# A hybrid encoder layer on one core: x parked in eight pieces, row factors broadcast from a column over the identity

## The reference

```python
h = rmsnorm(x, g_mix_pre)
q_a, k_a, v_a, q_r, k_r, v_r, g_r, gate_a, gate_r = split_in(h @ w_in)
o_a = sink_attention(...)          # 8 heads of 64, window of 2 chunks, sinks
o_r = head_group_norm(retention(...)) * silu(g_r)     # 4 heads, keys 128, values 256
merged = sigmoid(gate_a) * (o_a @ w_branch_attn) + sigmoid(gate_r) * (o_r @ w_branch_ret)
x = x + rmsnorm(merged @ w_out, g_mix_post)
h = rmsnorm(x, g_ffn_pre)
f = (silu(h @ w_ffn_gate) * (h @ w_ffn_up)) @ w_ffn_down      # hidden 2816
x = x + rmsnorm(f, g_ffn_post)
x = x + (p @ w_ple_proj) * sigmoid(x @ w_ple_gate)
```

## Time and profile before

| | |
|---|---|
| median of three runs | 1070.39 us (1069.06 to 1074.13) |
| the profiled execution | 1072.61 us, of it in the span 1070.8 us |
| busy: TensorE, VectorE, ScalarE, GpSimd | 1031.8, 509.0, 333.2, 127.6 us |
| mean granted clock of TensorE | 0.982 |
| chain that ended last, shares | PE 85%, DVE 6%, issue 3%, DMA 3%, ACT 1%, POOL 1% |
| DMA | 88.63 MB, mean 83 GB/s |

### The profile page before, as it was taken

One profiled execution on the slowest core, in us unless ns is written; L12 is line 12 of the kernel. 1 busy time (PEld: TensorE's weight loads), 2 busy tenths in 40 slices (PEclk: granted clock), 3 DMA queues, 4 the chain that ended last, 5 costly groups with the idle time before them and its releaser, 6 DMA issues.

```text
span 1070.8 us, 19780 instructions
## 1 busy us (share of the span) xinstructions
PE 1031.8 (96%) x7428; PEld 996.9 (93%) x7428; DVE 509.0 (48%) x869; ACT 333.2 (31%) x490; POOL 127.6 (12%) x148
## 2 busy tenths in 40 slices
PE   7999999999999999989969999999999999999797
PEld 6899899898999999989958999999999999999697
DVE  5544676666566433243276443332233444323842
ACT  5224434334334322123333222221123222222232
POOL 0221212122100000100222111100011111011000
PEclk9999999999999999989989999999999999999799
DMA  6732212212221323523221223222332222223132
GB/s 170 229 91 77 67 46 69 61 52 59 69 65 59 90 71 90 151 72 98 78 59 40 79 82 94 74 67 81 93 99 78 78 80 84 69 81 98 40 101 66
DMA packets 163817, 88.63 MB, mean 83 GB/s; under 512 B 14224, under 2 KB 162096, under 8 KB 163648
## 3 DMA queue, kind: packets, MB, share of 16 engines
q1 hardware_dynamic: 160256, 79.19, 25.7%
q0 software_dynamic: 1632, 7.23, 2.0%
q10 hardware_dynamic: 1888, 1.64, 0.5%
HBM read 82.08 MB, written 6.03 MB: 82 GB/s over the span
## 4 chain that ended last, share of the span: by engine, by line
PE 85%; DVE 6%; issue 3%; DMA 3%; ACT 1%; POOL 1%; DVEq 0%; SPq 0%; ACTq 0%; POOLq 0%
PE acc L467 77%; DMA raw<-in_w_in 2%; PE small L618 2%; PE small L633 1%; DMA raw<-in_w_branch_ret 1%; DVE wide L1412 1%; DVE wlo L1101 1%; PE small L661 1%; PE small L665 1%; DVE yl L1428 1%; PE small L663 1%; ACT whi L790 1%; PE small L570 0%; ACT prob L850 0%; PE small L673 0%
## 5 line engine op out<-in xcount | busy, mean ns | idle before, releaser
L1101 DVE TENSOR_TENSOR wlo<-raw,whi 128x1024 fp32r<-128x1024 f32 (+3 forms) x156 | 180.5, 1157 | 337.7 <-ACT whi L790 337.4
L790 ACT ACTIVATE whi<-raw 128x1024 fp32r<-128x1024 f32 (+3 forms) x156 | 153.1, 982 | 436.2 <-PE acc L467 418.9
L467 PE MATMUL acc<-yh,whi 128*128 128x288 f32 x960 | 209.0, 299 | 18.0 <-DVE yl L1428 10.5
L467 PE MATMUL acc<-yh,wlo 128*128 128x288 f32 x960 | 207.9, 298 | 0.0
L467 PE MATMUL acc<-yl,whi 128*128 128x288 f32 x832 | 179.2, 297 | 0.0
L467 PEld LDWEIGHTS acc<-yh,whi 128*128 128x128 f32 x960 | 155.6, 191 | 21.5 <-DVE yl L1428 12.2
L467 PE MATMUL acc<-xh,whi 128*128 128x288 f32 x736 | 163.9, 304 | 3.0 <-DVE wlo L1101 2.9
L467 PE MATMUL acc<-xl,whi 128*128 128x288 f32 x736 | 158.0, 296 | 0.0
L467 PE MATMUL acc<-xh,wlo 128*128 128x288 f32 x736 | 157.5, 295 | 0.0
L467 PEld LDWEIGHTS acc<-yh,wlo 128*128 128x128 f32 x960 | 155.5, 191 | 0.0
L467 PEld LDWEIGHTS acc<-yl,whi 128*128 128x128 f32 x832 | 135.5, 191 | 0.0
(11 more groups left out here) (218 smaller groups left out, 1115.2 us busy)
## 6 DMA issues: line engine op xcount, KB each, us to landing
raw<-in_w_in SPq DMA_DIRECT2D x92, 256.0 KB, 3.1
raw<-in_w_ffn_gate SPq DMA_DIRECT2D x44, 256.0 KB, 3.1
raw<-in_w_ffn_up SPq DMA_DIRECT2D x44, 256.0 KB, 3.2
raw<-in_w_ffn_down SPq DMA_DIRECT2D x48, 192.0 KB, 2.4
raw<-in_w_branch_ret SPq DMA_DIRECT2D x16, 256.0 KB, 2.8
raw<-in_w_out SPq DMA_DIRECT2D x16, 256.0 KB, 2.8
raw<-in_w_ple_gate SPq DMA_DIRECT2D x16, 256.0 KB, 3.0
x_scratch<-x_t POOLq DMA_DIRECT2D x1, 2304.0 KB, 15.5
```

What stands on the lines that cost most here:

```text
L467: ins = nc.tensor.matmul(acc[:, a, hf, 0:HALF], w[:, s, at:at + P], x(k)[:, hf * HALF:(hf + 1) * HALF], start=first and n == 0 and m == 0, ...
L790: nc.scalar.activation(whi[:, s, 0:n], raw[:, s, 0:n], ACT.Copy).then_inc(hi_ready, 1)
L1101: nc.vector.tensor_tensor(wlo[:, s, 0:n], raw[:, s, 0:n], whi[:, s, 0:n].bitcast(F32), ALU.subtract).then_inc(lo_ready, 1)
```

## The change

Two things change. The first is how x is parked: eight transfers, one for each tile, instead of one, issued later in GpSimd's list, and the reload of tile k waits for k units of the second merge stage instead of none. With it, the loads of p and of the caches go ahead of `power(0)`, behind a wait for x's last quarter. The second is the row factor: TensorE uses a column of `rstd`, read 128 times with a step of zero, as the stationary operand and the identity as the moving one. The product has the same values, since its k-th partition holds `rstd[k]` in every column.

```diff
             def row_factor(n):
 
+                pe.wait_ge(rstd_ready, n + 1)
                 for r in range(RT):
                     size = P if r < RT - 1 else DEC
-                    pe.wait_ge(diag_ready, RT * n + r + 1)
-                    ins = nc.tensor.matmul(small[:, r * P:r * P + size], ones[0:size, :],
-                                           diag[0:size, P * r:P * r + size], start=True, stop=True)
-                    ins.then_inc(bcast_done, 1)
+                    ins = nc.tensor.matmul(small[:, r * P:r * P + size], rstd[0:size, r:r + 1].to_broadcast([size, P]),
+                                           ident[0:size, 0:size], start=True, stop=True)
+                ins.then_inc(bcast_done, 1)
...
-                act.wait_ge(bcast_done, RT * (n + 1))
+                act.wait_ge(bcast_done, n + 1)
...
                 if t == 0:
-                    act.wait_ge(x_saved, 16)
+                    act.wait_ge(x_saved, 16 * KD)
...
-                dve.wait_ge(rstd_ready, n + 1)
-                for r in range(RT):
-                    size = P if r < RT - 1 else DEC
-                    nc.vector.tensor_scalar(diag[0:size, P * r:P * r + size], ident[0:size, 0:size],
-                                            rstd[0:size, r:r + 1], None, ALU.mult).then_inc(diag_ready, 1)
...
-            power(0)
+            pool.wait_ge(x_in[QUARTERS - 1], 32)
             pool.dma_start(p_row[:, 0:RT - 1, :], p_p[0, 0].rearrange("(r p) n -> p r n", p=P)).then_inc(p_in, 16)
             pool.dma_start(p_row[0:DEC, RT - 1, :], p_s[0, 0]).then_inc(p_in, 16)
             pool.dma_start(ck_row[:, :], cache_k[0, 0].rearrange("n h d -> n (h d)")).then_inc(cache_in, 16)
             pool.dma_start(cva[:, :], cache_v[0, 0].rearrange("n h d -> n (h d)")).then_inc(cache_in, 16)
+            power(0)
...
-            pool.wait_ge(xt_copied, KD)
-            pool.dma_start(scratch, x_t[:, :, :].rearrange("p k n -> p (k n)")).then_inc(x_saved, 16)
+
+            def save_x(k):
+
+                if k == 0:
+                    pool.wait_ge(xt_copied, KD)
+                pool.dma_start(scratch[:, k * ROWS:(k + 1) * ROWS], x_t[:, k, :]).then_inc(x_saved, 16)
+
...
                     head_job(t, h, slot)
+                    if isinstance(h, int):
+                        save_x(t + 2)
                     pieces(2 * t + 1, r, rslot)
...
             pool.wait_ge(tables_in, 32)
+            save_x(0)
+            save_x(1)
             head(0, None, 0, None)
...
-            pool.wait_ge(unit_done, U_MRG2)
-            pool.wait_ge(x_saved, 16)
+            pool.wait_ge(x_saved, 16 * KD)
             for k in range(KD):
+                pool.wait_ge(unit_done, U_MRG2 + k)
                 pool.dma_start(res[:, k, :], scratch[:, k * ROWS:(k + 1) * ROWS]).then_inc(x_back, 16)
```

More of the change, by code:

```diff
@@ L293, in encoder_layer @@
         assert e_at + slab + ROWS * 4 <= split_at
-        diag = tb
         acc = ctx.enter_context(nc.psum_tensor("acc", [P, 2, 2, 512], F32))
@@ L318, in encoder_layer @@
         x_saved, x_back = sem("x_saved"), sem("x_back")
-        squares_ready, var_ready, rstd_ready, diag_ready = (
-            sem("squares_ready"), sem("var_ready"), sem("rstd_ready"), sem("diag_ready"))
+        squares_ready, var_ready, rstd_ready = sem("squares_ready"), sem("var_ready"), sem("rstd_ready")
         bcast_done, rb_ready, sums_done = sem("bcast_done"), sem("rb_ready"), sem("sums_done")
@@ L1160, in _ @@
                 if k == 1:
-                    dve.wait_ge(bcast_done, RT)
+                    dve.wait_ge(bcast_done, 1)
                 nc.vector.tensor_copy((ta, tb)[k][:, :], small[:, 1024 * (k % 2):1024 * (k % 2) + ROWS]).then_inc(xt_copied, 1)
```

## The result

The changed kernel takes 1062.28 us in the median of 4 runs (1061.99 to 1062.63), the kernel before 1070.52 in the 4 runs beside them (1069.06 to 1074.13). The ratio is 0.9925, 95% interval 0.9911 to 0.994: 8.2 us less. The two profiled executions took 1072.61 and 1061.99; the trace accounts for the 10.8 us between their spans, which is more than the medians differ by.

A forecast was written before the change was run, and what follows sets the result against it. TensorE, busy 1031.8 of 1070.8 us, bounds the kernel; only its pauses and low clock can pay. Parking 2.8, reload 5.9 and row factors 1.1 sum to 9.8 us off the 1070.39 median: 1060.6, eight-in-ten range 1057.0 to 1066.0.

The forecast's parts named there:

- Reload: Late place, w_branch_ret load at 445.7 us: staged reloads save 3.5 us pause plus 2.4 low clock, 5.9 us.
- The price of 0.9 us per piece: Second merge: each of eight reload pieces delayed the late weight load by 0.9 us, also used for head 0.
- Row factors: Four row factors: dropping 20 VectorE multiplications and their hand-over saves 0.45, 0.4, 0 and 0.3, sum 1.1 us.
- The weight load with a step of zero: Row factors: cost taken as 0; the rival that zero-step loads are slow, up to 4.5 us, 1065.1, chance 0.05.
- Parking: Early place, w_in load at 31.6 us: moving x away saves 1.4 us pause plus 1.4 low clock, 2.8 us.
- Nothing is gained: Start: issuing loads of p and the cache ahead of power(0) gains nothing, cost 0 to 0.3 us.
- the deadline of 40.9: Early place: ScalarE's slot is free from 40.9 us; the w_in load, landing at 39.7, would come before that.
- The tables alone: Rival at the early place: tables alone hold the w_in load, leaving 7.0 us of gain, 1063.4; chance 0.08.
- The change did what it says: Rival denying this: the loads are late by themselves, only 1.1 us gain left, 1069.3; chance 0.04.
- Weight loads don't meet pieces one by one: Rival claiming they do: TensorE waits 2.6 us at three of four second-merge columns, 1068.4; chance 0.04.
- Head 0 was not starved: Rival claiming parking starves head 0: six stalls of 2.8 us, 16.8 us, 1077; chance 0.03.
- the rule that spoke against cutting: Skill page on x's transfers: 2.0 us fixed plus bytes at 436 GB/s; eight pieces need 21.4 us, one 7.4.

The follow-up runs named there:

- e4: Changed kernel with all eight reloads of x issued at once when the first merge stage ends; 1069.04 us, ratio 0.9991 to the kernel before.
- e3: Changed kernel with x parked whole in one transfer right behind the tables, loads of p still early; 1062.66 us, ratio 0.9938 to the kernel before.
- e1: Changed kernel with the old row factor (diagonals by VectorE, ones as stationary operand); 1063.65 us, ratio 0.9952 to the kernel before.
- e2: Kernel before with the new row factor alone, parking and reload as before; 1069.74 us, ratio 0.9998 to the kernel before.
- e12: Repeat of e5 (changed kernel with the old start), timed beside the unchanged changed kernel; 1063.18 us, ratio 0.9945 to the kernel before.
- e5: Changed kernel with the old start: loads of p and caches behind power(0), x whole behind the tables; 1063.54 us, ratio 0.9942 to the kernel before.
- e6: Changed kernel with the old start, but x in eight transfers one behind the other at the old place; 1063.41 us, ratio 0.9943 to the kernel before.
- e10: Kernel before, unchanged, run again for a second profile; 1069.99 us, ratio 1.0008 to the kernel before.
- e9: Changed kernel, unchanged, timed again; 1062.94 us, ratio 0.9942 to the kernel before.
- e7: Changed kernel with loads of p and caches behind power(0) again, x still in pieces in head 0; 1063.96 us, ratio 0.9949 to the kernel before.
- e11: Changed kernel with x parked as one transfer in front of head 0; 1062.84 us, ratio 0.9943 to the kernel before.
- e8: Changed kernel with the reload in two groups of four, at start and middle of the second merge; 1063.42 us, ratio 0.9939 to the kernel before.

## Why the prediction was right, and its mis-sized term

**Reload: right, a little low.** Forecast 5.9; 6.1 between the traces, 6.4 between e4 and e3. The step "the first two meet the load that was late: 4.9 us" holds: the first w_branch_ret load takes 5.2 us in the changed kernel, and ScalarE's slot, not the data, sets the start. The price of 0.9 us per piece was at the low end (0.9 to 1.2), with no consequence.

**Row factors: right by the traces.** Forecast 0.45, 0.4, 0, 0.3; the traces give 0.5, 0.3, 0, 0.3. The medians agree (e1 against e3 1.0 us) but are no finer than that, and e2 shows no gain. The weight load with a step of zero, the unknown of this part, costs nothing. L538 after, from the view of one line (min, median, max ns; first and last start):

```profile
L538 PEld LDWEIGHTS small<-tab,rstd x40: 182/190/192, 27.8 to 984.9; 128*128 128x128 f32 x32, 64*128 64x128 f32 x8
```

The weight loads that it replaces took 182/192/192 ns in the kernel before.

**Parking: mis-sized.** The step that failed is "1.4 + 1.4 = 2.8 us saved". As a reading of that one execution it was near: 3.1 between the two traces. As a forecast of medians it was not. Six profiles have this stall: pauses of 1.37 (before), 1.01 (e2), 0.79 (e12), 0.52 (e5), 0.44 (e6) and 0.29 (e10), and only behind the longest did the clock fall. The load comes at 47.5 to 48.3 in all of them; TensorE's last transpose ends between 49.34 and 49.96, with the start of the execution, so the pause is the difference of two times that move apart and together by half a microsecond. In the medians e12 - e9 is 0.2 us and e5 - e7 is -0.4, in the profiled executions of the same pairs 1.2 and 0.6: the term is 0 to 1 us. The prediction noted that the profiled execution was 2.2 us above the median, and took that execution's terms off the median all the same; there the miss lies.

With 0.5 in place of 2.8, the late place at 6.4 and the factors at 1.2 the sum is 8.1, and 1070.4 - 8.1 = 1062.3 is the time. That it meets it to a tenth is luck. The repeat gives 6.1 (7.1 against e10), e3 gives 6.8 with both stalls gone and the new factor, and e4, which lacks only the late term, gives 0.5 where this sum has 1.7. The late term is the one that stands well above what the medians can tell.

**Two readings inside it were wrong too.** "Nothing is gained" for p's loads: e3 shows that moving them ahead of power brings the tables and the load forward enough. The load issued at 31 us took 14.9 us in e5, 11.7 in e3 and 4.9 after the change. And the deadline of 40.9 was 4.8 us too strict, so that cover was there for things I held to be necessary: with p's loads early, e3 shows that x need not leave its place, and e11 that in front of head 0 one transfer does as well as eight in steps.

**The rivals.** The tables alone don't hold the load (7.1 and 9.4 us to landing before, 5.0 and 5.9 now). The change did what it says. Weight loads don't meet pieces one by one: from 452 to 462 TensorE is busy for 9.90 of 10.00 us. Head 0 was not starved. On the rule that spoke against cutting: one transfer of 2304 KB landed in 7.7 us in e11 and each piece in 2.9. An estimate by the formula of the Trainium skill, "DMA: Bandwidth & Descriptors", "Anatomy of one DMA — SWDGE (gpsimd) path", is 7.4 and 2.68 for these, so this case's traces agree with both figures; but the sum of eight, 21.4 us, was paid nowhere. In e6, with eight pieces in flight, ScalarE's split could start at 47.50, and at 47.77 in e5 beside the whole: pieces in flight overlap.

**The spread.** The kernel before spreads over 4.6 to 6.1 us each time, the changed one over 0.6. e2, with both stalls, spreads over 7.3, and e4, with the late one alone, over 6.4; the kernels without the late stall (e1, e3, e5 to e9, e11, e12) over 0.6 to 2.8, in 4 to 6 runs each. So most of the spread belongs to the late place, where the pause is 3.5 to 4.6 us in the profiles and the lower clock costs 1.1 to 2.6 on top (72 products in 10.99 to 12.26 us, against 9.62 to 9.85 undisturbed). The cost goes with how long the clock stays at 0.50: from about 458.0 to 464.8 us in the kernel before and 455.6 to 462.4 in e4, but only from 458.2 to 461.6 in e2, whose pause of 4.5 us is as long as that of e4. Why it comes back sooner in one execution than in another stays open.

## What to carry to other kernels

When a load is late, ask which bytes other queues issued around it, and release those in steps; how coarse the steps may be is set by when the consumer wants the data, and that is later than when the slot in front of it is free. A stall that one profile shows may be a draw and not a size: the early one cost 3.1 us there and 0.5 to 1.3 (pause and slower products) in the five other profiles that have it. Look whether a pause and the clock behind it come back in a second execution before they are put into a sum. Of several edits made together, one line may carry the gain: here the wait of the reload gives 6.4 us of a gain of 6 to 8.

## What the hardware showed that I had not expected

A weight load of 256 KB, 3.1 us at the median, took 7.9 us with four transfers of 288 KB that GpSimd had issued beside it (e8), and 10.5 to 11.5 with eight (before, e10, e2, e4): 0.9 to 1.2 us for each. Cut or whole made no difference to their neighbours: at the early place four weight loads took 13.3 us in the median in e5 and in e6 alike. The same 2304 KB took 7.7 us in front of head 0, where they met no weight load on its way for long, 12.4 behind the tables and 14.3 to 15.5 behind p's loads and the tables: its time was decided by its neighbours. A pause of 1.37 us at the early place was followed by the lower clock, one of 1.01 at the same place was not.
